# Two transformer blocks on one core: the head squares of the second mixer summed as a hi and a lo part, the lo part made by GpSimd between the taps of the convolution

## The reference

```
u = cg * hc
u = lax.conv_general_dilated(u, conv_w[:, None, :], ..., padding=[(1, 1)], feature_group_count=CONV_WIDTH)
y_conv = bg * (u + conv_b)
...
h = h_fwd + h_bwd
h = h * lax.rsqrt(jnp.mean(h * h, axis=-1, keepdims=True) + EPS) \
    * head_gain.astype(jnp.float32).reshape(H, 1, DV)
...
y_mlstm = jax.nn.sigmoid(o) * h
return jnp.concatenate([y_conv, y_mlstm], axis=-1) @ w_out
```

## Time and profile before

| | |
|---|---|
| median of 3 runs | 803.46 us (803.43 to 803.59) |
| profiled execution, its time | 803.71 us |
| profiled execution, its span | 801.8 us |
| mean granted clock of TensorE | 0.999 |
| PE busy | 788.4 us (98%) |
| DVE busy | 533.1 us (66%) |
| ACT busy | 429.8 us (54%) |
| POOL busy | 27.1 us (3%) |

### The profile page before, as it was taken

The page is one execution under the profiler, slowest core; times in us unless marked ns, Lnnn a source line. Parts: engine busy times, 40 slices in busy tenths (PEclk is TensorE's granted clock), DMA queues, the critical chain, the costliest instruction groups (busy, mean ns, idle before and its releaser), DMA issues.

```text
span 801.8 us, 12188 instructions
## 1 busy us (share of the span) xinstructions
PE 788.4 (98%) x4716; PEld 694.2 (87%) x4716; DVE 533.1 (66%) x625; ACT 429.8 (54%) x565; POOL 27.1 (3%) x31
## 2 busy tenths in 40 slices
PE   8999999999999999999999999999999999999997
PEld 8989988888888888888888887999988888888885
DVE  7865557766666666866666566766987756656665
ACT  6557557544445447744544446565556654454444
POOL 0000100000000000000000000002320000000000
PEclk9999999999999999999999999999999999999999
DMA  8633333645546453665545554452454665554531
GB/s 329 233 116 105 126 128 112 246 171 206 183 184 209 166 200 107 238 220 197 200 168 208 181 185 159 150 191 105 158 165 147 224 221 169 203 189 179 208 105 53
DMA packets 20797, 141.16 MB, mean 176 GB/s; under 512 B 2448, under 2 KB 2704, under 8 KB 4384
## 3 DMA queue, kind: packets, MB, share of 16 engines
q1 hardware_dynamic: 20192, 138.65, 48.8%
q0 software_dynamic: 576, 2.10, 0.8%
HBM read 139.69 MB, written 1.05 MB: 176 GB/s over the span
## 4 chain that ended last, share of the span: by engine, by line
PE 90%; DVE 4%; ACT 3%; issue 1%; DMA 1%; POOL 1%; SPq 0%; DVEq 0%; ACTq 0%
PE ps L1446 88%; DVE wlo L998 1%; ACT whi L675 1%; PE ps L1452 1%; DMA raw<-wstream 1%; DVE x L1196 0%; ACT squared L690 0%; DVE xa L1009 0%; POOL arena L656 0%; DVE arena L1412 0%; PE ps L1681 0%; POOL arena L653 0%; PE ps L1653 0%; DVE arena L1423 0%; DVE xg L1191 0%
## 5 line engine op out<-in xcount | busy, mean ns | idle before, releaser
L1446 PE MATMUL ps<-xa,whi 128*128 128x512 f32 (+2 forms) x1744 | 488.3, 348 | 0.6 <-DVE ytmp L1364 0.6
L1446 PE MATMUL ps<-xa,wlo 128*128 128x256 f32 (+1 forms) x1376 | 383.1, 282 | 0.0
L998 DVE TENSOR_TENSOR wlo<-raw,whi 128x2048 fp32r<-128x2048 f32 x128 | 293.1, 2291 | 83.6 <-ACT whi L675 83.6
L1446 PEld LDWEIGHTS ps<-xa,whi 128*128 128x128 f32 x1744 | 302.6, 188 | 44.3 <-issue 1.9
L1446 PEld LDWEIGHTS ps<-xa,wlo 128*128 128x128 f32 x1376 | 258.7, 188 | 1.1
L675 ACT ACTIVATE whi<-raw 128x2048 fp32r<-128x2048 f32 x128 | 244.2, 1908 | 6.9 <-PE ps L1446 6.9
L1446 PE MATMUL ps<-whi,hhi 128*128 128x512 f32 x240 | 93.8, 391 | 0.0
L1446 PE MATMUL ps<-whi,hlo 128*128 128x512 f32 x240 | 93.7, 390 | 0.0
L1446 PE MATMUL ps<-wlo,hhi 128*128 128x512 f32 x240 | 93.5, 390 | 0.0
L869 ACT ACTIVATE hhi<-arena 128x512 fp32r<-128x512 f32 x30 | 19.0, 633 | 89.0 <-PE ps L1446 82.5
L855 ACT ACTIVATE arena<-ps 128x512 f32<-128x512 f32 x33 | 19.7, 596 | 87.5 <-PE ps L1446 87.2
(11 more groups left out here) (214 smaller groups left out, 530.8 us busy)
## 6 DMA issues: line engine op xcount, KB each, us to landing
raw<-wstream SPq DMA_DIRECT2D x128, 1024.0 KB, 4.8
gain_row<-rows_in POOLq DMA_DIRECT2D x4, 512.0 KB, 4.0
x<-x_in SPq DMA_DIRECT2D x2, 512.0 KB, 4.1
raw<-wstream SPq DMA_DIRECT2D x2, 512.0 KB, 5.7
out<-x SPq DMA_DIRECT2D x4, 256.0 KB, 2.0
xg<-const_in SPq DMA_DIRECT2D x1, 912.0 KB, 11.7
small<-small_in SPq DMA_DIRECT2D x1, 152.0 KB, 6.0
arena<-meta_in SPq DMA_DIRECT2D x1, 64.0 KB, 4.7
```

Of the source, the lines that this page charges most:

```text
L998: nc.vector.tensor_tensor(wlo[slot][:], raw[slot][:], whi[slot][:].bitcast(F32), ALU.subtract).then_inc(lo_ready, 1)
L1446: return nc.tensor.matmul(o, lhsT, rhs, start=start, stop=stop, skip_group_check=True)
```

## The change

The four heads of the second block's mixer get the treatment of the first block. `squares()` on ACT now writes `ysq`, waits for it, and copies it as fp32r into `sq_hi`. GpSimd gets a step `low_squares` after each `ml_apply`, which writes `sq_lo`; for that its list of taps becomes a walk over `SECOND`. PE's one float32 matmul per head becomes two fp32r matmuls, on `sq_hi` and `sq_lo`. In the first block the same code is only moved into the two helpers.

```diff
+            def low_squares(key):
+                pool.wait_ge(sq_hi_ready, SQ_AT[key] + 1)
+                if SQ_AT[key]:
+                    pool.wait_ge(sq_summed, SQ_AT[key])
+                nc.gpsimd.tensor_tensor(sq_lo, ysq[:, key[1] % 2, :], sq_hi.bitcast(F32), ALU.subtract).then_inc(sq_ready, 1)
...
-                    for c in range(4):
-                        pool.wait_ge(tap_ready, c + 1)
...
+                    for kind, c in SECOND:
+                        if kind == "ml_apply":
+                            low_squares(("ml_norm", c))
+                        if kind == "tap":
+                            pool.wait_ge(tap_ready, c + 1)
...
             def squares(key, bank):
-                nc.scalar.activation(ysq[:, key[1] % 2, :], ps[:, bank, 0:SEQ], ACT.Square).then_inc(sq_ready, 1)
+                n = SQ_AT[key]
+                nc.scalar.activation(ysq[:, key[1] % 2, :], ps[:, bank, 0:SEQ], ACT.Square).then_inc(sq_out, 1)
+                act.wait_ge(sq_out, n + 1)
+                if n:
+                    act.wait_ge(sq_summed, n)
+                nc.scalar.activation(sq_hi, ysq[:, key[1] % 2, :], ACT.Copy).then_inc(sq_hi_ready, 1)
...
                 if kind == "ml_norm":
+                    total = ps[:, ML_BANK[i], SEQ:2 * SEQ]
+                    pe.wait_ge(sq_hi_ready, SQ_AT[(kind, i)] + 1)
+                    mm(total, ones_r, sq_hi, True, False)
                     pe.wait_ge(sq_ready, SQ_AT[(kind, i)] + 1)
-                    mm(ps[:, ML_BANK[i], SEQ:2 * SEQ], ones, ysq[:, i % 2, :], True, True).then_inc(sq_summed, 1)
+                    mm(total, ones_r, sq_lo, False, True).then_inc(sq_summed, 1)
```

More of the change, by code:

```diff
@@ L639, in _ @@
                 if n == 0:
[L641 to L645, removed]
-                if n == 2:
-                    for c in range(4):
-                        pool.wait_ge(tap_ready, c + 1)
[L650 to L658, removed]
@@ new lines, in _ @@
+                    for kind, i in FIRST:
+                        if kind in ("fox_apply", "sb_apply"):
+                            low_squares((kind[:-5] + "norm", i))
+                if n == 2:
+                    for kind, c in SECOND:
[3 more added lines that the diff above has]
+                            pool.wait_ge(tap_ready, c + 1)
+                            if c:
+                                pool.wait_ge(conv_ready, c)
+                            for tap in (1, 2):
+                                nc.gpsimd.tensor_scalar(mtap[:, tap - 1, :], mu[:, tap:tap + SEQ], vec("conv_w", 4 * tap + c), None,
+                                                        ALU.mult).then_inc(tap_product, 1)
+                            pool.wait_ge(tap_product, 2 * c + 2)
+                            nc.gpsimd.tensor_tensor(mtap[:, 0, :], mtap[:, 0, :], mtap[:, 1, :], ALU.add).then_inc(tap_sum, 1)
+                            pool.wait_ge(tap_sum, c + 1)
+                            nc.gpsimd.tensor_tensor(mw[:, c % 2, :], mw[:, c % 2, :], mtap[:, 0, :], ALU.add).then_inc(conv_ready, 1)
@@ L828, in _ @@
                     act.wait_ge(fox_applied if kind == "fox_apply" else sb_applied, i + 1)
[L829 to L834, removed]
+                    squares((kind[:-5] + "norm", i), 6 + i % 2)
                 if kind == "sb_score":
@@ L975, in _ @@
                     act.wait_ge(ml_applied, i + 1)
-                    squares((kind, i), ML_BANK[i])
+                    squares(("ml_norm", i), ML_BANK[i])
                 if kind == "ml_norm":
```

## The result

| | before | after |
|---|---|---|
| median of 22 runs each, alternating on the same chips | 803.51 us | 804.47 us |
| ratio after to before, with its 95% interval | | 1.0015 (1.0009 to 1.0022) |
| profiled execution, its time | 803.71 us | 804.94 us |
| its span | 801.8 us | 803.0 us |

The changed kernel is slower by 0.15%, 1.2 us by the ratio and 0.96 us by the medians. That is less than the 0.2% that the prediction took as the least that can be told, but the interval does not hold 1.

What follows compares the result with a forecast made beforehand. PE's stream was taken to bound the kernel, with DVE and GpSimd deciding ahead of 573.01 us. +0.55 (head 0) + 0.44 (head 1) - 0.36 (PE's gain) = +0.63 us, giving a median of 804.1 us, range 803.0 to 804.6.

Steps and rivals of the forecast that it cites:

- What bounds the kernel: Whole kernel: PE's stream, 90% of the span; ahead of 573.01 in the mixer DVE and GpSimd count, behind it PE.
- PE's gain: Mixer sums: fp32r pairs save 0.18 us per head; -0.36 us for heads 2 and 3, nothing for heads 0 and 1.
- ACT's copies: Four copies behind the mixer's squares: costed at nothing; without cover, at most 0.53 us each.
- Head 0: GpSimd's low part at 552.86, ahead of DVE's weight split at 552.92: split late, +0.55 us; 0 if the split goes first.
- Head 1: GpSimd's low part at 567.19 starts after DVE's second scaling and delays the L1427 behind it: +0.44 us, bounds 0 and 0.57.
- Heads 2 and 3: Low parts behind 573.01: DVE about 0.44 us late at head 2, but 0 at PE, at most 0.13; head 3 0.
- The sum: Whole change: +0.55 for head 0, +0.44 for head 1, -0.36 for PE's gain, together +0.63 us.
- The case of a long subtraction: Rival at heads 0 to 2: GpSimd's subtraction itself takes 2.66 us and DVE stands still; +6.4, 809.8 us, chance 0.04.
- the one from the sum to the chances: Whole kernel: 0.2%, 1.6 us, taken as the least measurable; faster 0.02, same 0.93, slower 0.05.
- The rival that was put aside: TensorE's clock around unit 10: granted clock 1.00 before, longest wait growing from 0.59 to 1.94 us; not priced, no chance given.

Runs made afterwards that it cites:

- no_low: Changed kernel without GpSimd's low parts in the mixer, PE summing the hi part twice instead; 803.23 us, ratio 0.9995 to the kernel before.
- heads23: Changed kernel with hi and lo parts for heads 2 and 3 only, heads 0 and 1 keeping the float32 matmul; 803.32 us, ratio 0.9995.
- held: Changed kernel with GpSimd's low parts of heads 0 to 2 waiting until VectorE's additions ahead of the next weight split are done; 803.31 us, ratio 0.9993.
- long_wait: Kernel before with three small chained memsets on VectorE ahead of the gate products in slot 8, no low parts; 805.46 us, +1.79.
- filled: Changed kernel with nine fp32r matmuls, their result unread, put into PE's wait ahead of unit 10; 804.41 us, ratio 1.0008 to the kernel before.
- again_2: The changed kernel, unedited, run a third time to see its two groups; median of nine times 805.86 us, +2.16 against the kernel before.

## Why the prediction was wrong, and where it was right

**What bounds the kernel.** Right. The loss appears at the one wait ahead of unit 10, the gain at heads 2 and 3, each in the size of its own row.

**PE's gain.** Right: 0.36 us by the sum, 0.40 in `no_low` and 0.33 in `heads23`, by the lag.

**ACT's copies.** Right, nothing: `no_low` has them and its mixer is shorter than before's by PE's gain.

**Head 0.** Right: +0.55 forecast, 0.54 in the split's row (2.83 against 2.29). The choice between GpSimd and the split, which was left to 0.06 us, went the way of the sum; `held` shows the other side of it. The trace agrees with the rule of the Trainium skill (SBUF — State Buffer, Who interferes with whom) that whichever issues first has the shared pair for its whole instruction, at head 0 (GpSimd at 553.34, the split at 553.39) as in `held`; at head 1 one of the two had it whole, but by the recorded starts not the first.

**Head 1.** The mechanism was right and the size was not. The sum took GpSimd as waiting for the second scaling (0.44 us); in the trace it went ahead of it, and the pair of scalings took 0.57 us longer. The recorded start of that scaling is 568.17, 0.03 us before GpSimd's 568.20, and still it was VectorE that waited. So the recorded start alone doesn't say who is first; a difference of a few hundredths can go either way. 0.57 was the upper bound of this term.

**Heads 2 and 3.** Right: 0 at PE. At head 2 the scalings are late by the same 0.57 us (1.47 us for the two at 582.12), and PE shows no new wait at the output projection. Head 3's low part came at 595.06 and met a cast and a subtraction, not the weight split that the text named; the subtraction took 0.84 us instead of 0.42, and none of it reached PE.

**The sum.** +0.63 forecast, +0.76 and +0.77 in the mixer of two profiles; the missing 0.13 is head 1's term (0.57 and not 0.44). The case of a long subtraction did not come, L632 took 0.73 to 0.74 us at heads 0 to 2; the 2.36 us that it had for head 1 does not follow from the rows as it stands (569.85 - 567.54 - 0.13 is 2.18), which changes neither the sum nor a chance.

**The step that failed** is the one from the sum to the chances. It took 0.2% as about what a measurement can tell, and so called 0.63 us no change with a chance of 0.93. The 22 times of before all lie within 0.62 us of their median, and 22 pairs of runs told 0.15% from nothing. The sum itself spoke for slower, and with the measured interval, 0.0006 to 0.0007 or about 0.5 us to either side, a loss of 0.63 us would still have stood clear of 1, by a little. The measured 804.47 us lies inside the stated 803.0 to 804.6; what failed is that a range from a gain to a loss was read as no change.

**The rival that was put aside.** "TensorE's clock is no rival that I can price": the granted clock was 1.00 in both stretches with the waits of before, and the text stopped there, although it forecast that the longest wait would grow from 0.59 to 1.94 us. With that wait 20 of 52 executions took some 1.3 us longer: in the profile of one, the clock is halved right behind it, and 1.5 us are lost. The upper group moves the median of the changed kernel from 804.42 (lower group) to 804.47 in the first comparison, and to 805.86 where six of nine fell into it. `long_wait` shows the group without GpSimd, `filled` shows it gone with the wait filled, and `again_2` shows the clock. That every execution of the upper group has its half clock at this place is inferred from the one that was profiled; `filled` shows another place, the start, in one execution.

**The whole.** 0.77 us of the 0.96 between the medians are the change's delay in the mixer. The rest is a matter of where in its spread each median lies, the upper group among it, and is not split further. In the first comparison even the lower group's median is 0.91 above before.

**A version that keeps the gain.** `held` and `heads23` are each 0.36 us below the kernel before by their medians, with -0.36 and -0.33 in their profiles' mixers. Both intervals hold 1 by a little (0.9984 to 1.0002 and 0.9986 to 1.0004), so by time alone neither is shown to be faster.

## What to carry to other kernels

Work that is put on GpSimd between VectorE's instructions is not free because GpSimd is idle 96% of the time: look at what VectorE does in the microsecond in which it starts, and whether VectorE is on the chain there. The order of arrival decides who pays, so a wait that lets the long VectorE instruction begin first can take the loss away: here 0.77 us lost in the mixer became 0.36 us gained by the profiles. And before a wait of TensorE is called cheap because it is one microsecond among hundreds, ask how long it becomes: here one of 1.8 us put the clock behind it at stake too.

## What the runs showed of the hardware

- A VectorE instruction that was caught by GpSimd was late by the overlap less 0.13 to 0.17 us: 0.57 us at the scaling (overlap 0.74), 0.54 us at the split (overlap 0.68), 0.42 us at the last head's subtraction in the changed kernel (0.84 us at 595.38, GpSimd until 595.93, overlap 0.55). The other way round GpSimd ended 0.59 or 0.60 us behind VectorE's end, at heads 0 and 1 of `held` and at 595.06 below.
- The scaling at 568.17 lost against GpSimd at 568.20, while the cast at 595.04 kept its 0.30 us against GpSimd at 595.06, which took 0.87:

```profile
595.04 0.30 DVE L1026 CAST ya<-ytmp 128x256 fp32r<-128x256 f32 x1
595.38 0.84 DVE L1027 TENSOR_TENSOR ya<-ytmp,ya 128x256 fp32r<-128x256 f32 x1
```

- A TensorE wait of 1.80 us ahead of unit 10 was followed by the half clock in one profile of the changed kernel (`again_2`) and by the full clock in another of the same program, the one after the change; one of 2.2 us in the profile of `long_wait` was followed by the full clock. None of the 77 executions of the seven other kernels with a wait of 0.6 to 1.6 us there lay 1.3 us above its group.
- At the start of the program the clock fell in one profile (`filled`), about 1 us behind a wait of 1.26 us for the first loads; in the other profiles that wait was 0.9 us at most and the clock stayed full. A wait of 1.4 us near 37 us, in every profile, the one of before included, was followed by the full clock. So the length of a wait does not tell by itself, and no run here shows what else decides.
